# Later adaLN groups divided between TensorE and VectorE separately for each role

## What is computed

```python
mod = silu(c) @ w_ada + b_ada                          # (B, 6*2048), c is one row per batch element
shift1, scale1, gate1, shift2, scale2, gate2 = split(mod, 6)
h = rmsnorm(x, g1) * (1 + scale1) + shift1
q_sb, k_sb, v_sb, q_dl, k_dl, v_dl, gate_pre = split(h @ w_in)
o_sb = stick_breaking_attention(q_sb, k_sb, v_sb)      # 8 heads: cumulative product over keys
o_dl = dilated_window_attention(q_dl, k_dl, v_dl)      # 12 heads: windowed softmax, dilations 1, 4, 16
mixed = (sigmoid(..) * (o_sb @ w_proj_sb) + sigmoid(..) * (o_dl @ w_proj_dil)) @ w_out
x = x + gate1 * mixed
h2 = rmsnorm(x, g2) * (1 + scale2) + shift2
x = x + gate2 * ((silu(h2 @ w_ffn_gate) * (h2 @ w_ffn_up)) @ w_ffn_down)
out = rmsnorm(x, g_final)
```

## Time and profile before

| | |
|---|---|
| time, median of 3 runs | 2223.72 us (2222.96 to 2231.47) |
| the profiled execution | 2224.84 us; its slowest core spans 2223.2 us |
| odd cores (role 1), span | 2217.9, 2220.0, 2220.5, 2223.2 us |
| even cores (role 0), span | 2209.4, 2205.1, 2201.8, 2202.1 us |
| TensorE matmul, busy on core 7 | 2076.0 us (93%), 13388 instructions |
| TensorE weight load, busy | 1177.9 us (53%) |
| VectorE, ScalarE, POOL, busy | 935.8, 596.2, 122.3 us |
| HBM read | 407.67 MB, 194 GB/s over the span |

### The profile page before, as it was taken

How to read it: one execution, slowest core, us unless ns; L and a number is a source line. 1 busy time by engine, 2 the same in 40 slices (tenths; PEclk the granted TensorE clock), 3 DMA queues, 4 the chain that set the end, 5 groups by cost and what they waited for, 6 DMA issues and landing times.

```text
span 2223.2 us, 34880 instructions; the slowest of 8 cores (2201.8 to 2223.2 us)
## 1 busy us (share of the span) xinstructions
PE 2076.0 (93%) x13388; PEld 1177.9 (53%) x13388; DVE 935.8 (42%) x1375; ACT 596.2 (27%) x1090; POOL 122.3 (6%) x235
## 2 busy tenths in 40 slices
PE   3499889999999999989999979999999999999997
PEld 1267556465646755654444434444444444444476
DVE  2362642888889882244445435222221110011124
ACT  2131321555555552141111136200000000011111
POOL 1100000000000000001101100000000000100000
PEclk9799999999999999999999989999999999999998
DMA  9998551221111335539778895355775444476647
GB/s 155 175 165 158 98 110 26 39 39 20 27 32 24 68 71 102 91 54 188 137 144 155 160 229 139 76 101 93 132 133 96 87 95 85 86 161 144 141 121 216
DMA packets 75895, 243.07 MB, mean 109 GB/s; under 512 B 7420, under 2 KB 45132, under 8 KB 58316
## 3 DMA queue, kind: packets, MB, share of 16 engines
q0 software_dynamic: 33264, 190.89, 48.1%
q1 hardware_dynamic: 35404, 41.26, 6.6%
q10 hardware_dynamic: 7056, 8.60, 1.2%
HBM read 407.67 MB, written 23.92 MB: 194 GB/s over the span
## 4 chain that ended last, share of the span: by engine, by line
PE 80%; DMA 8%; DVE 5%; ACT 3%; issue 2%; another core or an unknown queue 0%; DVEq 0%; POOL 0%; POOLq 0%; ACTq 0%; SPq 0%
PE ps L470 77%; PE ps L920 2%; DMA a_ada_65<-w_ada 2%; DMA b_ada_253<-w_ada 2%; DMA b_xq_336<-xT 1%; ACT b_h2T_331 L474 1%; DMA b_mslot_328<-w_mod 1%; DVE b_h2T_331 L478 1%; DVE b_hT_252 L592 1%; DMA vl<-b_V_35_264 1%; DMA a_ada_64<-w_ada 1%; DMA xnewT<-b_xq_336 1%; ACT L474 0%; DMA b_ring_259<-w_ffn_up 0%; DVE b_mslot_328 L1167 0%
## 5 line engine op out<-in xcount | busy, mean ns | idle before, releaser
L470 PE MATMUL ps<-b_hT_252,b_ring_258 128*128 128x512 bf16 (+1 forms) x752 | 172.5, 375 | 5.5 <-DVE b_hT_252 L592 5.3
L470 PE MATMUL ps<-b_hT_252,b_ring_260 128*128 128x512 bf16 (+2 forms) x624 | 132.4, 363 | 3.7 <-DVE b_hT_252 L592 3.1
L470 PE MATMUL ps<-b_hT_252,b_ring_261 128*128 128x512 bf16 (+2 forms) x592 | 131.4, 370 | 3.7 <-DVE b_hT_252 L592 3.7
L470 PE MATMUL ps<-b_h2T_331,b_ring_272 128*128 128x472 bf16 (+1 forms) x576 | 122.4, 362 | 3.5 <-ACT b_h2T_331 L474 3.5
L470 PE MATMUL ps<-b_h2T_331,b_ring_258 128*128 128x472 bf16 (+1 forms) x576 | 122.6, 363 | 0.0
L470 PEld LDWEIGHTS ps<-b_hT_252,b_ring_258 128*128 128x128 bf16 x752 | 73.6, 100 | 88.2 <-issue 15.9
L470 PE MATMUL ps<-b_h2T_331,b_ring_261 128*128 128x472 bf16 (+1 forms) x576 | 119.6, 361 | 0.0
L470 PE MATMUL ps<-b_hT_252,b_ring_259 128*128 128x512 bf16 (+1 forms) x464 | 105.9, 373 | 7.5 <-DVE b_hT_252 L592 3.1
L470 PE MATMUL ps<-b_h2T_331,b_ring_259 128*128 128x464 bf16 (+1 forms) x512 | 106.3, 361 | 0.3 <-DMA b_ring_259<-w_ffn_up 0.3
L470 PE MATMUL ps<-b_h2T_331,b_ring_260 128*128 128x464 bf16 (+1 forms) x512 | 106.3, 361 | 0.0
L470 PEld LDWEIGHTS ps<-b_hT_252,b_ring_260 128*128 128x128 bf16 x624 | 58.8, 99 | 67.4 <-issue 10.4
(11 more groups left out here) (1864 smaller groups left out, 3713.7 us busy)
## 6 DMA issues: line engine op xcount, KB each, us to landing
b_ring_258<-w_in POOLq DMA_DIRECT2D x9, 1024.0 KB, 11.1
b_ring_261<-w_in POOLq DMA_DIRECT2D x9, 1024.0 KB, 11.4
b_ring_260<-w_in POOLq DMA_DIRECT2D x8, 1024.0 KB, 10.8
b_ring_259<-w_in POOLq DMA_DIRECT2D x8, 1024.0 KB, 14.9
b_mslot_327<-w_mod POOLq DMA_DIRECT2D x16, 512.0 KB, 7.2
b_mslot_328<-w_mod POOLq DMA_DIRECT2D x16, 512.0 KB, 7.7
b_ring_272<-w_ffn_gate POOLq DMA_DIRECT2D x7, 1024.0 KB, 10.7
a_ada_63<-w_ada POOLq DMA_DIRECT2D x6, 1024.0 KB, 11.2
```

Source lines behind the costliest of these rows:

```text
L470: P.op("pe", lambda e: e.matmul(out_ap, lhsT=lhsT, rhs=rhs, start=start, stop=stop, skip_group_check=True), reads=reads, pwrites=[b], inc= ...
```

## The change

`ON_PE` becomes a pair: 12 for role 0, 16 for role 1. In role 1 it is now the four stick-breaking rounds that ask for groups, two each, and the dilated rounds ask for none. So groups 8 to 15 go to TensorE there, and VectorE keeps 16 to 19 in the merge and 20 to 23 later. Role 0 keeps its division. The host lays out `w_mod` per role. The `mslot` tiles (one for role 1, two for role 0) are taken ahead of `mT`, the first of them in a gap behind the `sg` tiles, which `o_qkv0` is enlarged to hold. That leaves room for a third early `w_out` panel in role 1; three remain late.

```diff
-ON_PE = 12
+ON_PE = (12, 16)
-    o_qkv0 = region(qb + kb_ + vb)
+    o_qkv0 = region(max(qb + kb_ + vb, 8 * 2048 + 4096))
-            if gi < ON_PE:
+            if gi < ON_PE[role]:
-        if r.kind == "dil":
+        for _ in range((r.kind == "dil", 2 * (r.kind == "sb"))[role]):
             mod.want(8 + nmod)
             nmod += 1
-    for gi in range(ON_PE, 20):
+    for gi in range(ON_PE[role], 20):
         mod.want(gi, apart=True)
-    early = Space([(o_work, o_hT), (o_qkv0 + 8 * 2048, o_odl), (o_end + 6144, size)])
+    early = Space([(o_qkv0 + 8 * 2048, o_odl), (o_work, o_hT), (o_end + 6144, size)])
     ring.free.append(A.at("pslot", o_end, [128, 3072], BF16))
     ring.pump()
+    mslots = [A.at("mslot", early.must(4096), [128, 2048], BF16) for _ in range((20 - ON_PE[role]) // 4)]
     mT = A.at("mT", early.must(16 * OWN * 2), [128, 16, OWN], BF16)
...
     mod.spread()
-    mslots = [A.at("mslot", early.must(4096), [128, 2048], BF16) for _ in range(2)]
     mod.ring.free += mslots
```

More of the change, by code:

```diff
@@ L1164, in emit @@
             gi, n, hs, *of = self.steps.pop(0)
-            if gi >= ON_PE:
+            if gi >= ON_PE[role]:
                 w, c = hs[0].t.ap[:, slice(*of[1])], 4 * gi + n
@@ L1194, in on_pe @@
         def on_pe(self):
-            return self.steps[0][0] < ON_PE
+            return self.steps[0][0] < ON_PE[role]
         def needs(self):
@@ L1270, in build_role @@
             r.rv = col(r.vc0)
-        if r.kind == "dil":
+        for _ in range((r.kind == "dil", 2 * (r.kind == "sb"))[role]):
             mod.want(8 + nmod)
             nmod += 1
-    assert 8 + nmod == ON_PE
+    assert 8 + nmod == ON_PE[role]
     gate_req = []
@@ L2106 @@
         "w_ada": np.ascontiguousarray(tiles(f(w_ada)[0][:, :2 * D], 128).reshape(16, 2, 128, D).transpose(0, 2, 1, 3)).reshape(16, 128, 2 * D),
-        "w_mod": np.concatenate([
-            f(w_ada)[0][:, 2 * D:].reshape(2, 8, 128, 16, 512).transpose(3, 0, 2, 1, 4).reshape(16, 2, 128, 4096)[:ON_PE - 8],
-            f(w_ada)[0][:, 2 * D:].T.reshape(16, 2, 2, 128, D).transpose(0, 1, 3, 2, 4).reshape(16, 2, 128, 4096)[ON_PE - 8:]]), "b_ada": f(b_ada)[0], "b_adaT": colT(f(b_ada)[0], 96),
+        "b_ada": f(b_ada)[0], "b_adaT": colT(f(b_ada)[0], 96),
         "g1T": colT(f(g_norm1)[0], 16), "g2T": colT(f(g_norm2)[0], 16),
@@ L2117 @@
     }
+    w_later = f(w_ada)[0][:, 2 * D:]
+    on_pe = w_later.reshape(2, 8, 128, 16, 512).transpose(3, 0, 2, 1, 4).reshape(16, 2, 128, 4096)
+    on_dve = w_later.T.reshape(16, 2, 2, 128, D).transpose(0, 1, 3, 2, 4).reshape(16, 2, 128, 4096)
+    w_mods = [np.concatenate([on_pe[:n - 8], on_dve[n - 8:]]) for n in ON_PE]
     quad = shared["w_in"][[c // 256 for c in QUAD]].reshape(4, 128, 4, 1024)
@@ L2125 @@
         m = dict(shared)
+        m["w_mod"] = w_mods[r]
         xs = np.concatenate([x[b, :t1][::-1], x[b, t1:]], axis=0)
```

## The result

The changed kernel took **2212.77 us** (median of four runs, 2212.03 to 2214.37), beside 2224.64 for the kernel before: a ratio of 0.9942, 95% interval 0.992 to 0.9964. Run again later beside the last experiments it took 2209.0 us, ratio 0.9923 (0.9906 to 0.994). So it is faster by 0.6 to 0.8%, some 13 to 17 us, just beyond what a measurement of this kernel can tell from no change. Every ratio leaves out executions in which half of the chip ran slower, and sets the others beside those of the kernel before measured with them.

The account below looks back on a forecast made before the run. Role 1's core 7 set the time, with VectorE pacing stick-breaking rounds and a TensorE stall in the output projection; +2 +2 -3.2 +0 -8 = -7.2 us from the 2223.72 median gave 2216.5 us, range 2209.5 to 2227.

Parts of the forecast that it names:

- before the first round: Before role 1's first stick-breaking round: two groups come, one goes, partly in TensorE's gaps; +2 us, bounds 0 and +3.2.
- stick-breaking rounds: Three rounds each gain 3.2 us of groups, covered by VectorE's pace and 4.8 idle us; +2, bounds 0 and +9.6.
- dilated rounds: Two groups leave role 1's dilated rounds, where TensorE is nearly full, so their time comes back; -3.2 us, bounds -3.2 and 0.
- merge: 16 steps leave VectorE and 16 transfers leave POOL's queue, where nothing waits for them; 0 us.
- output projection: The tail term: earlier evictions and late w_out panels shorten TensorE's stall; -8 us, bounds -3 and -13.
- feed-forward: Feed-forward layer to the end: the prediction's sum held no term for it.
- rival 1: The output projection's stall disappears, all 20.6 us go and role 0 is last; 2210 us, chance 0.22.
- The tail: Output projection: no or two w_mod steps left, evictions and late panels earlier, stall-ending refill at about 1297; -8 us.
- Rival 2: Leftover w_mod steps on the one slot hold evictions to about 1254, tail gains 4, not 8; 2220.5 us, chance 0.12.
- rival 3: Tail bound by bytes and turns alone, refill still at about 1305; sum +0.8, 2224.5 us, chance 0.10.
- Rival 4: TensorE bounds the stick-breaking rounds, each added group costs its 1.60 us; sum +9.8, 2233.5 us, chance 0.11.

Follow-up runs that it names:

- again: The changed kernel once more, unaltered, run beside the last experiments: 2209.0 us, ratio 0.9923.
- asked in dilated: Changed kernel, but role 1 asks for its eight groups two at a time in the four later dilated rounds, none in stick-breaking rounds: ratio 0.9949.
- The third group: Changed kernel with twelve groups on TensorE in role 1, three behind each stick-breaking round's panels instead of two: ratio 0.9929.
- The split alone: Change's split (eight groups on TensorE in role 1) in the memory layout of before, two VectorE slots, two early w_out panels: ratio 0.9945.
- later panels: First two feed-forward panels behind the merge held until the projection's 17th and 21st group, both roles: ratio 0.9927 on changed, 0.9989 on before, 0.9914 with the twelve groups spread.
- spread: Changed kernel, twelve TensorE groups in role 1, asked for two, none, three, three, two, two from the third round on: 2210.26 us, ratio 0.9946.
- idle groups: Kernel before plus two groups of identity products, results thrown away, ahead of and in role 1's stick-breaking rounds but the last: ratio 0.9998.

## Why the prediction was right and where it was wrong

The time lay in the range, and the direction was right. The sum was -7.2 us and the mean of role 1's cores moved by -14.1 (again: -14.2), so I gave most of the chance to the wrong side of 0.5%. The time itself moved by 11.9, less than the mean, because the last core decides: in the profiled execution core 1 came late to its first scan (397.6) and took 117.6 us for its projection. By the prediction's own steps:

| step | forecast (bounds) | changed | again |
|---|---|---|---|
| before the first round | +2 (0 to +3.2) | +4.0 | +4.9 |
| stick-breaking rounds | +2 (0 to +9.6) | -4.7 | -4.2 |
| dilated rounds | -3.2 (-3.2 to 0) | -4.6 | -4.2 |
| merge | 0 | 0.0 | 0.0 |
| output projection | -8 (-13 to -3) | -9.1 | -11.3 |
| feed-forward | 0 | +0.3 | +0.5 |

*The stick-breaking rounds* are the step that failed, and with 6.7 us nearly the whole miss (the other steps cancel to 0.2). That the time lay in the range all the same is no merit of this step: the range reached low because of rival 1. I argued that VectorE sets the pace and that 3.2 us of groups fit into 4.8 idle us, and stopped at 0 as the best case. The row that would have carried the bound below nothing lay in the trace: the idle time at a round's end was followed by 7 to 10 us at half clock. There, and where TensorE was full at the lower clock inside a round, the round grew, so VectorE does not set the pace throughout. Work put into the idle time was paid back by the clock; I had excluded a gain without a reason. Not all of the 4.7 us is shown to be the clock's: 1.5 of them lie in the fourth round, which kept 1.1 of these with the clock down at its start (asked in dilated). The rule of the Trainium skill that I weighed there ("Perfetto Trace Analysis", section "Identifying the Most-Contended Engine") would have made this term 0. The third group at no cost agrees with it that there was room, but the gain is beyond it. Another page of the Trainium skill, "TensorE: Matmul & The Clock Gate", section "HAM oscillation — how this bites in real kernels", would have pointed at it: it counts half of the time at the lower level as lost. For the third round (6.8 us) that is an estimate of 3.4 us; measured were 2.0.

*Before the first round* my bounds were too narrow. The place of the pair was right (320 to 345 us), and moving it gave 4.9 us back (394.4 to 389.5). TensorE's window there, on core 7 of before, shows how little room it had:

```profile
310.00:350.00 40.00, 37.08 (x238) 19.22 (x237) 14.34 (x18) 9.40 (x14) 1.05 (x2) 0.96 0.54 122
```

The group that left was worth nothing, since it stood in a gap (two groups in the same gap left the part at 389.5 us); so the full 3.2 us should have been the value. The rest is idle time and clock around it that the runs do not part.

*The dilated rounds* gave back 1.0 to 1.4 more than two groups. Four groups there took 154.6 us (asked in dilated), no more than two in the kernel before. So the stage isn't a plain sum of its groups. The clock behind the last scan differed too: on core 7 it was up with the four groups, down for 6.8 us before and for 10.2 us in the changed kernel. What the remainder is stays open.

*The tail* went as forecast in its mechanism, and the refill that ends the stall came where it was forecast: 54.7 us behind the projection's start (1292.3 and 1237.6), where 1297 with a start near 1242.8 made 54.2. The split alone shows that taking the w_mod steps out did it. The rule of the Trainium skill in "DMA: Bandwidth & Descriptors", section "Queues, rings and completion order", would have left -3. The later panels agree with it that POOL's panels hold back SP's tiles; but the panels themselves waited behind the steps, so they ended 14.5 us earlier too, and the measured term was -9 to -11. With later panels, where the stall is gone, the steps still cost 10.3 us over both stages (976.1 and 965.8). Whether VectorE's late evictions or POOL's late panels made the larger part is not shown.

*The rivals.* Rival 1 came close by its floor: role 0 is now last in some executions. But its price for the stall, the whole 20.6 us, was wrong: with the stall gone entirely, 3.6 (before), 5.1 (changed) or 0.4 us (spread) were left of it. Rival 2 (steps left over) and rival 3 (bytes alone) did not happen. Rival 4 falls by the third group, of which only the first round shows a part of the price.

## What to carry to other kernels

Before charging for work that moves onto TensorE, look at the granted clock just behind its idle stretches: filler work that closes such a stretch can cost less than nothing, and work put where the engine is already full costs its whole time. Look also at where the clock falls next, since it can fall elsewhere instead. A stall's length is not its price: follow the late data to its next reader, and count both stages together. When two roles end within 1% of each other, a gain in one is worth only the distance to the other.

## What the runs showed of the hardware that I had not expected

The granted clock fell in the same places round after round (494 to 504, 610 to 617 and 723 to 730 us on core 7 of before) and stayed up there when 128 one-column matmuls were added in each round, even ones whose results nobody reads. On some cores, and with the idle groups on all four in one round, it fell for 3.4 us inside a round instead. Cores with the same program in the same execution differed in this. At half clock a full TensorE lost half the time (1.7 of 3.4 us); at the rounds' ends, where it was partly idle, some 7 us of low clock went with 2 us of a longer round (112.7 against 110.6); and behind the last scan it showed no clear cost: 149.4 us to the merge on core 5 of the changed kernel, with 10 us of it, and 150.2 on the two cores of the spread run that had none.
